# Single blocks' sums over partitions by two products of split parts with ones, the first norm's sum in the middle of the second gate tile

## The reference, cut to what matters

```python
def finish_layer(h, att, cv, p, w_out, g_ffn, w_gate_up, w_down, g_ple, w_ple_gate, w_ple_proj):
    h = h + jnp.concatenate([att, cv], axis=-1) @ w_out
    u = rms_norm(h, g_ffn)
    gate, up = jnp.split(u @ w_gate_up, 2, axis=-1)
    h = h + (jax.nn.silu(gate) * up) @ w_down
    g = jax.nn.sigmoid(rms_norm(h, g_ple) @ w_ple_gate)
    return h + g * (p @ w_ple_proj)
```

## Time and profile before

| | |
|---|---|
| runs of the kernel before | 2595.4 us median of 3 (2593.06 to 2597.45) |
| profiled execution, its own time | 2595.5 us |
| its span | 2593.7 us |
| busy in the span | PE 2571.5, DVE 1853.9, ACT 1266.1, POOL 597.2 us |
| mean granted clock of PE | 0.999 |
| blocks 0, 1 and 2 in `finish` | from 750 us to 1936 us |

### The profile page before, as it was taken

How to read it: one execution, slowest core, us unless ns; L and a number is a source line. 1 busy time by engine, 2 the same in 40 slices (tenths; PEclk the granted TensorE clock), 3 DMA queues, 4 the chain that set the end, 5 groups by cost and what they waited for, 6 DMA issues and landing times.

```text
span 2593.7 us, 39929 instructions
## 1 busy us (share of the span) xinstructions
PE 2571.5 (99%) x13924; PEld 2497.0 (96%) x13924; DVE 1853.9 (71%) x3393; ACT 1266.1 (49%) x2283; POOL 597.2 (23%) x663
## 2 busy tenths in 40 slices
PE   9999999999999999999999999999999999999999
PEld 8999998999989999999999999999999999999999
DVE  4555579988888888777766877789538766666557
ACT  5344368888864323444334443423446443443465
POOL 6222211121121333323233333233200010111000
PEclk9999999999999999999999999999999999999999
DMA  5667798888677888898888898898896565665675
GB/s 204 215 214 244 237 361 272 280 290 273 201 242 250 289 302 282 303 349 286 307 320 312 281 335 300 303 325 314 294 348 190 162 188 183 187 197 181 198 238 186
DMA packets 316883, 677.12 MB, mean 261 GB/s; under 512 B 37485, under 2 KB 174573, under 8 KB 316141
## 3 DMA queue, kind: packets, MB, share of 16 engines
q1 hardware_dynamic: 295324, 603.78, 69.8%
q0 software_dynamic: 21360, 70.80, 7.7%
HBM read 512.19 MB, written 164.29 MB: 261 GB/s over the span
## 4 chain that ended last, share of the span: by engine, by line
PE 83%; DVE 6%; DMA 5%; ACT 2%; issue 2%; SPq 1%; POOL 0%; DVEq 0%; ACTq 0%; POOLq 0%
PE psum L198 51%; PE psum L2571 24%; PE psum L1556 2%; PE psum L1581 2%; DMA x<-in_w_gu 2%; PE psum L1543 1%; PE psum L1544 1%; DVE wres L3136 1%; DMA a_cr<-in_cache 1%; DVE y L3183 1%; DMA x<-in_w_down 1%; ACT wres L3004 1%; DVE ul L685 0%; POOL wres L628 0%; DMA rstd<-in_w_in 0%
## 5 line engine op out<-in xcount | busy, mean ns | idle before, releaser
L198 PE MATMUL psum<-uh,wres 128*128 128x416 f32 x3936 | 1119.2, 356 | 6.4 <-DVE wres L3136 2.6
L198 PEld LDWEIGHTS psum<-uh,wres 128*128 128x128 f32 x3936 | 736.8, 188 | 20.7 <-DVE wres L3136 5.7
L198 PE MATMUL psum<-ul,wres 128*128 128x416 f32 x1968 | 688.0, 350 | 0.0
L3004 ACT ACTIVATE wres<-x 128x1024 fp32r<-128x1024 f32 (+2 forms) x234 | 268.6, 1148 | 640.6 <-PE psum L198 536.2
L198 PE MATMUL psum<-wres 128*128 128x416 f32 x2304 | 447.9, 352 | 2.2 <-DVE wres L3136 2.2
L198 PEld LDWEIGHTS psum<-wres 128*128 128x128 f32 x2304 | 430.3, 188 | 9.9 <-DVE wres L3136 3.6
L2571 PE MATMUL psum<-wres 128*128 128x416 f32 x2104 | 426.0, 351 | 0.7 <-DVE c_top L2490 0.6
L2571 PEld LDWEIGHTS psum<-wres 128*128 128x128 f32 x2104 | 393.3, 188 | 6.3 <-issue 1.6
L198 PEld LDWEIGHTS psum<-ul,wres 128*128 128x128 f32 x1968 | 370.4, 188 | 6.6 <-issue 1.4
L3183 DVE SCALAR_TENSOR_TENSOR y<-c_top,vec,y 128x416 f32<-128x416 f32 (+1 forms) x600 | 339.2, 633 | 0.8
L1737 ACT ACTIVATE wres<-c_top 128x512 fp32r<-128x512 f32 (+1 forms) x302 | 181.3, 602 | 127.2 <-PE psum L2571 46.8
(11 more groups left out here) (314 smaller groups left out, 3628.0 us busy)
## 6 DMA issues: line engine op xcount, KB each, us to landing
x<-in_w_gu SPq DMA_DIRECT2D x132, 512.0 KB, 5.3
wres<-w_gu_lo SPq DMA_DIRECT2D x88, 512.0 KB, 6.1
c_top<-w_gu_sums SPq DMA_DIRECT2D x136, 256.0 KB, 3.2
x<-in_w_down SPq DMA_DIRECT2D x48, 704.0 KB, 6.6
w_gu_sums<-c_top POOLq DMA_DIRECT2D x60, 512.0 KB, 6.2
w_gu_lo<-wres SPq DMA_DIRECT2D x44, 512.0 KB, 6.4
c_top<-in_w_gu POOLq DMA_DIRECT2D x88, 256.0 KB, 5.8
wres<-w_down_lo SPq DMA_DIRECT2D x32, 704.0 KB, 7.5
```

What stands on the lines that cost most here:

```text
L198: mm = nc.tensor.matmul(out, w[wp](kw), u[up](ku), start=first and n == 0 and j == 0, stop=last and n == len(kts) - 1 and j == 2)
L3004: nc.scalar.activation(whi[v % 2][:, 0:kts, :], raw[v % 2][:, 0:kts, :], ACT.Copy).then_inc(hi_done, 1)
```

## The change

Each sum over partitions of the single blocks (six norms and eight totals of the convolution) is now two fp32r products with ones, of a high and of a low part of the vector of sums, in place of one fp32 product. The high part is made by ACT (`sum_high`, `total_high`), the low part by DVE (`sum_low`, `total_low`). `cv_sum_up` adds the four tiles by three TENSOR_TENSOR in a row in place of the TENSOR_REDUCE. `norm(b, 0)` moves from behind G0 into the middle of G1: after 12 of G1's 24 products. The code of ACT and DVE for the norm (root, reciprocal) stays in G0's. The waits' counts follow. `ones_r` is the tile of ones read as fp32r.

```diff
+    def ends_block(u):
+
+        return u["kind"] == "D" and u["half"] == 1 and u["m"] == KD - 1
...
+        sum_hi, sum_lo = c["hx"][:, 3 * KP, :], c["hx"][:, 3 * KP + 2, :]
+        total_hi, total_lo = (c["between"][:, (5 + e) * N + 4 * KH * P:(6 + e) * N + 4 * KH * P] for e in range(2))
+        ones_r = c["ones"][:, :].bitcast(F32R)
...
+            def sum_high(b, i):
+                act.wait_ge(sum_out, sum_count(b, i, KD - 1))
+                nc.scalar.activation(sum_hi, ssum[:, :], ACT.Copy).then_inc(sq_out, 1)
+
+            def total_high(n, i):
+                act.wait_ge(cv_sum, (CT + 1) * total_count(n, i) + CT - 1)
+                nc.scalar.activation(total_hi, csum[:, :], ACT.Copy).then_inc(cv_sum, 1)
...
                 if last_tile(u) and b < SINGLE:
+                    sum_high(b, 0)
                     act.wait_ge(p_in, 16 * (b + 1))
                     nc.scalar.activation(ph[:, :, :], p[:, :, :], ACT.Copy).then_inc(p_hi, 1)
...
+                    for i in range(2):
+                        if early(u) and u["f"] == STEPS[early(u)]["total"][i]:
+                            total_high(early(u), i)
                     act.wait_ge(left, u["left0"] + 1)
                     nc.scalar.activation(sig[:, :], g[:, :], ACT.Sigmoid).then_inc(sig_out, 1)
...
                 elif kind == "D" and u["half"]:
+                    if late(u) and u["m"] in (1, 6):
+                        total_high(late(u), int(u["m"] == 6))
                     tile_out(b, 1, u["m"], V_GPLE, u["left0"] + 1)
...
+                    if u["m"] == KD - 1:
+                        sum_high(b, 1)
...
             def cv_sum_up(n, i, src):
-                nc.vector.tensor_reduce(out=csum[:, :], in_=src[:, :, :].rearrange("p c n -> p n c"),
-                                        axis=AX.X, op=ALU.add).then_inc(cv_sum, 1)
+                for ct in range(1, CT):
+                    if ct > 1:
+                        dve.wait_ge(cv_sum, (CT + 1) * total_count(n, i) + ct - 1)
+                    nc.vector.tensor_tensor(csum[:, :], csum[:, :] if ct > 1 else src[:, 0, :], src[:, ct, :],
+                                            ALU.add).then_inc(cv_sum, 1)
+
+            def total_low(n, i):
+                dve.wait_ge(cv_sum, (CT + 1) * total_count(n, i) + CT)
+                nc.vector.tensor_tensor(total_lo, csum[:, :], total_hi.bitcast(F32), ALU.subtract).then_inc(cv_sum, 1)
+
+            def sum_low(b, i):
+                dve.wait_ge(sq_out, sq_count(b, i, KD) + 1)
+                nc.vector.tensor_tensor(sum_lo, ssum[:, :], sum_hi.bitcast(F32), ALU.subtract).then_inc(sum_out, 1)
...
                     if last_tile(u) and b < SINGLE:
                         weight_low(v + 2)
+                        sum_low(b, 0)
...
-                for n, r in taps_of[v]:
+                for e, (n, r) in enumerate(taps_of[v]):
                     taps(n, r)
+                    if e == 0 and ends_block(u):
+                        sum_low(b, 1)
+                if not taps_of[v] and ends_block(u):
+                    sum_low(b, 1)
...
             def norm(b, i):
-                pe.wait_ge(sum_out, sum_count(b, i, KD - 1))
+                pe.wait_ge(sum_out, sum_count(b, i, KD))
                 if b or i:
                     pe.wait_ge(n_sd, 2 * b + i)
-                nc.tensor.matmul(ps_n[:, 0:N], c["ones"][:, :], ssum[:, :], start=True, stop=True).then_inc(n_mm, 1)
+                nc.tensor.matmul(ps_n[:, 0:N], ones_r, sum_hi, start=True, stop=False)
+                nc.tensor.matmul(ps_n[:, 0:N], ones_r, sum_lo, start=False, stop=True).then_inc(n_mm, 1)
 
             def cv_total(n, i):
-                pe.wait_ge(cv_sum, (n - 1) * 2 + i + 1)
-                nc.tensor.matmul(ps_c[:, 0:N], c["ones"][:, :], csum[:, :], start=True, stop=True).then_inc(cv_mm, 1)
+                pe.wait_ge(cv_sum, (CT + 1) * (total_count(n, i) + 1))
+                nc.tensor.matmul(ps_c[:, 0:N], ones_r, total_hi, start=True, stop=False)
+                nc.tensor.matmul(ps_c[:, 0:N], ones_r, total_lo, start=False, stop=True).then_inc(cv_mm, 1)
...
+                    elif kind == "G" and u["half"] == 0 and u["f"] == 1:
+                        passes(nc, out, w, U, [(k, k) for k in range(KD // 2)], True, False)
+                        norm(b, 0)
+                        mm = passes(nc, out, w, U, [(k, k) for k in range(KD // 2, KD)], False, True)
...
                 mm.then_inc(used, 1)
-                if kind == "G" and u["half"] == u["f"] == 0:
-                    norm(b, 0)
```

More of the change, by code:

```diff
@@ L1957, in last_pair @@
     u_hi, u_lo, sq_out, sum_out = (f[e] for e in ("u_hi", "u_lo", "sq_out", "sum_out"))
-    T0, Q0, A0 = 2 * SINGLE * KD, (2 * SINGLE + 1) * KD, (2 * SINGLE + 1) * (KD - 1)
+    T0, Q0, A0 = 2 * SINGLE * KD, (2 * SINGLE + 1) * KD + 2 * SINGLE, (2 * SINGLE + 1) * KD - 1
     n_mm, n_sd, n_r, NN = f["n_mm"], f["n_sd"], f["n_r"], 2 * SINGLE
@@ L2832, in tile_count, with sq_count, total_count @@
             return (2 * b + i) * KD + m
+        def sq_count(b, i, m):
+            return tile_count(b, i, m) + 2 * b + i
         def sum_count(b, i, m):
-            return (2 * b + i) * (KD - 1) + m
+            return (2 * b + i) * KD + m
+        def total_count(n, i):
+            return 2 * (n - 1) + i
         def sig_count(b, kind, n):
@@ L3202, in tile_out @@
                 if m:
-                    dve.wait_ge(sq_out, tile_count(b, i, m) + 1)
+                    dve.wait_ge(sq_out, sq_count(b, i, m) + 1)
                     if m >= 2:
@@ L3221, in first_sum @@
                 if m:
-                    dve.wait_ge(sq_out, tile_count(SINGLE, 0, m) + 1)
+                    dve.wait_ge(sq_out, sq_count(SINGLE, 0, m) + 1)
                     if m >= 2:
@@ L3291, in _ @@
                         hidden_low(b, u["half"], u["f"] - 1)
+                    for i in range(2):
+                        if early(u) and u["f"] == STEPS[early(u)]["total"][i]:
+                            total_low(early(u), i)
                     dve.wait_ge(sig_out, sig_count(b, "G", u["half"] * HF + u["f"] + 1))
@@ L3325, in _ @@
                             n = late(u)
+                            if m in (1, 6):
+                                total_low(n, int(m == 6))
                             if m == 0:
```

## The result

| | us |
|---|---|
| before | 2594.65 median of 6 (2592.46 to 2597.45) |
| changed | 2608.12 median of 6 (2605.63 to 2613.51) |
| ratio | 1.0047, 95% interval 1.0037 to 1.0058 |
| profiled execution of the changed kernel | 2613.5, span 2611.8 |

The kernel got slower by 0.47%, 12 us by the ratio, where 0.42% and 2606.4 us were forecast.

A forecast was written before the change was run, and what follows sets the result against it. PE, busy 99% of the span, was taken as the bound. The terms -4.2 + 0.4 + 0.2 + 11.0 + 3.6 = 11.0 us on 2595.5, less 0.1 for the median, gave 2606.4 us; range 2600.5 to 2610.5.

The forecast's parts named there:

- The cheaper sums: Single blocks: thirteen sums at 0.38 us in place of 0.70 gain 4.2 us; block 0's first norm loses cover, costing 0.4.
- The moved norm: Start of U1 in each block: PE stalls for late weights, 3.4 us in block 0, 3.8 in blocks 1 and 2, 11.0 together.
- The chain from root to weights: From the norm's last product to U1's start: steps in series, 5.77 us in blocks 1 and 2, 5.37 in block 0.
- the table load: ACT's load for the root or sigmoid runs ahead of the wait, counted as none; 1.28 us more each if not.
- The clock: At the three U1 stalls: PE's clock falls to half, 1.2 us lost each, 3.6 us together.
- The rival in which it holds: At U1: the three stalls come but PE's clock stays up; 7.4 us lost, 2602.8 us; chance 0.22.
- Block 1's first P: Norm behind block 1's first P: `sum_low` follows two taps, so PE waits 0 to 0.2 us; 0.2 taken.
- Block 2's backlog: U4's high part in block 2, with DVE behind on taps: the 0.8 us margin stays; counted 0, up to 1 us.
- Block 0 gives back part: Later in block 0: PE finds late low parts ready, taking up that block's 3.4 us; 2601.8 us; chance 0.07.

The follow-up runs named there:

- the version at 0.9981: Changed kernel with norm(b, 0) behind 6 of U0's 24 products and block 1's norm(1, 1) behind 6 products of the X unit; 2589.67 us, ratio 0.9981.
- the experiment with the early high part: Changed kernel with ACT making U1's high part before the root of the first norm in blocks 1 and 2; 2601.27 us, ratio 1.0029.
- the low part ahead of the taps: The version at 0.9981 with DVE making the sum's low part before the six taps at the end of block 1's last D; 2590.3 us, ratio 0.9979.

## Why the prediction was right, and where it was off

- *The cheaper sums, -4.2 us and +0.4 us.* Right in the chain: 0.38 us for each. As a time the gain stands by itself in no run: with the move undone nothing is left of it (1.0001), and the version at 0.9981 also waits less in block 0.
- *The moved norm, 11.0 us.* Right in mechanism and in size: 3.3, 3.7 and 3.7 us, 10.7 in all, against 3.4, 3.8 and 3.8. The chain from root to weights came within 0.05 us, the table load ran ahead of the wait, and moving the norm by 12 products moved the stalls by 2.25 us.
- *The clock, 3.6 us.* Right in direction, and between 3.2 us (by the profiles) and 5.3 us (by the mean clock of all runs, falls at other places with them), though not as thought. In the changed kernel's profile a fall costs the full 1.5 us, since it comes only behind the stall; in two other profiles it began inside the stall. Not every stall brings one: seven in ten did. The rival in which it holds was no case of its own; it holds or falls from one stall to the next.
- *Block 1's first P, 0.2 us.* This step failed, by the term for `sum_low` against PE's demand at 1474.34. The prediction let `sum_low` follow the first two of six taps after 1.2 to 1.8 us, at most a third of the 5.38 us of all six. But in the kernel before the first two are slower than the others, as the timeline of DVE cut down to them shows:

```profile
1472.10 2.17 DVE L3183 SCALAR_TENSOR_TENSOR y<-c_top,vec,y 128x416 f32<-128x416 f32 x2
```

  They end at 1474.27, and with 0.6 to 1.1 us for `sum_low` itself PE would have waited 0.5 to 1.0 us even there. The kernel with the norm behind U0, where POOL's additions lie beside the same taps as before, shows the whole of it in its timeline of DVE; PE's sum waits until 1478.24:

```profile
1474.99 2.16 DVE L3225 SCALAR_TENSOR_TENSOR y<-c_top,vec,y 128x416 f32<-128x416 f32 x2
1477.07 1.11 DVE L3183 TENSOR_TENSOR c_hx<-c_top,c_hx 128x416 fp32r<-128x416 f32 x1
```

  The second half of the error is that DVE's lateness was taken from one profile. In the nine profiles with split sums the waits there are 2.66, 0.40, 2.35, 2.25, 2.13, 1.42, 2.28, 1.17 and 1.27 us, 1.8 us in the mean, twice with a fallen clock behind them (the changed kernel, and the norm behind U0); in the two without, nothing. What is known is how: six taps take 3.46 us alone (the repeated changed kernel, at 1474.84) and 4.4 to 5.4 us while POOL adds, as two timelines of the changed kernel show, DVE's first:

```profile
1476.69 5.40 DVE L3225 SCALAR_TENSOR_TENSOR y<-c_top,vec,y 128x416 f32<-128x416 f32 x6
1482.02 0.58 DVE L3366 TENSOR_TENSOR z<-psum,z 128x416 f32<-128x416 f32 x1
```

POOL's of the same kernel, of a round's additions two of those beside the taps:

```profile
1477.45 0.97 POOL L1778 TENSOR_TENSOR c_top<-c_top 128x256 f32<-128x256 f32 x1
1478.50 0.97 POOL L1780 TENSOR_TENSOR c_top<-c_top 128x256 f32<-128x256 f32 x1
```

  DVE began to evict that last tile 4.4 us behind PE here, 1.0 us behind in the kernel before. In the five profiles in which POOL's additions lie beside the taps in front of that eviction it was 3.9 to 4.4 us late, in the other four 1.7 to 3.2. PE waits for the last low part of u once it is over 3.0 us. Why POOL's rounds so often fall there in the kernels with split sums is open.
- *Block 2's backlog, 0.* Right for the change; the experiment with the early high part shows that it is next, 2.2 us.
- *Block 0 gives back part (a rival with a chance of 0.07).* It came true for block 0. From the start of U0 to the first total PE took 269.6 us before (783.20 to 1052.80) and 271.6 in the profile after (786.83 to 1058.38), 2.0 us more, where norm, stall and clock there come to 0.4 + 3.3 + 1.5 = 5.2. So 3.2 us were given back. Behind U3 PE waits 3.6 us before and 1.6 in the changed kernel. It is not the move that takes those waits away: with split sums they are 1.6 to 3.6 us in the six profiles with the norm in G1 or behind U0 (3.1 with the move alone), and 0.1 us at most in the three with the norm behind G0 or 6 products into U0. Why is open. The baseline is one profile.

Summed anew: -4.2 + 0.4 + 10.7 + 3.2 + 1.8 = 11.9 us, against 12.2 (9.6 to 15.0) by the ratio. With 5.3 us for the clock it is 14.0, and block 0 gives back some 2 to 3 of them. So the forecast of 11.0 us rests on a stall that was right, and for the rest it was lucky: more falls of the clock and the waits at block 1's first P were made good by block 0. The profiled execution is 18 us above that of before. Of these 3.6 us had come up before block 0's U0 (786.83 in place of 783.20) and 2.4 us come behind block 2's last product, where the change does nothing. The other 12 us are the terms with four falls of the clock (6.0 us) and 2.7 us of waits in block 1, 15.6 us, less what block 0 gives back.

## What to carry to other kernels

A product that another engine waits for is placed by the chain behind it: root, reciprocal, eviction, sigmoid and the next weights' split were 5.7 us in a row, and 12 products of cover were 2.3. Read how long the chain from the product back to PE's next need is, and put the product at least that far ahead. A saving of 0.3 us on each of fourteen sums is lost by one or two late operands, so see that the new operand's producer is not the engine that is late, and time the very instructions in front of it: a mean over six taps hid that the first two were slow.

## What the runs showed of the hardware

The clock of PE may fall after PE has taken up work again: idle for 3.5 us until 1189.69, at 1.2 GHz only from about 1190.2. In the profile with the move alone it fell 1.4 us before the end of such a stall, and stayed down for 6.8 us in place of 3.4. Stalls of 3.0 to 3.5 us brought it down in seven of ten cases. Single waits of 0.8 and 1.2 us did so in none, one of 2.28 us did. Waits of 0.25, 0.23 and 1.44 us close together did; waits of 0.51, 0.23 and 0.95 us did in two profiles, and the same waits in a third (the low part ahead of the taps) did not. The Trainium skill, TensorE: Matmul & The Clock Gate, section "Why this matters for your kernels", wants no long gaps between bursts of matmuls; the runs agree, but show that several short waits close together can bring the clock down as one long one does, and that the same stall may or may not.

A TENSOR_REDUCE over four tiles of 416 columns took 3.2 us, three TENSOR_TENSOR in a row 1.8 us in most places and up to 2.8 us. A SCALAR_TENSOR_TENSOR of 416 columns took 0.65 us alone and 1.1 us beside an addition of POOL.
